# Softmax over the dilated groups on compact columns, with only the shares spread over the channels

## What is computed

```python
o = jnp.stack(outs, axis=2)
alpha = jax.nn.softmax(jnp.stack(lses, axis=2), axis=2)
o = (o * alpha[..., None].astype(o.dtype)).reshape(B, S, DIL_WIDTH)
return o * jax.nn.silu(g)
```

```python
w = jnp.exp(-DECAY_SCALE * jax.nn.sigmoid((w0 + jnp.tanh(wd) @ w_up).astype(f32)))
a = jax.nn.sigmoid((a0 + ad @ a_up).astype(f32))
kk = kk / jnp.maximum(jnp.linalg.norm(kk, axis=-1, keepdims=True), 1e-12)
k = k * (1.0 + (a - 1.0) * per_head(k_a))
```

## Time and profile before

| | |
|---|---|
| median of 3 runs | 2264.72 us (2263.03 to 2273.73) |
| the profiled execution | 2263.61 us, its span 2261.8 us |
| mean granted TensorE clock | 0.958 |
| PE busy | 2076.3 us (92%) |
| DVE busy | 956.5 us (42%) |
| ACT busy | 440.8 us (19%) |
| POOL busy | 239.7 us (11%) |

### The profile page before, as it was taken

The page is one execution under the profiler, slowest core; times in us unless marked ns, Lnnn a source line. Parts: engine busy times, 40 slices in busy tenths (PEclk is TensorE's granted clock), DMA queues, the critical chain, the costliest instruction groups (busy, mean ns, idle before and its releaser), DMA issues. The chain is left out here.

```text
span 2261.8 us, 31372 instructions
## 1 busy us (share of the span) xinstructions
PE 2076.3 (92%) x12841; PEld 1026.2 (45%) x12841; DVE 956.5 (42%) x1773; ACT 440.8 (19%) x877; POOL 239.7 (11%) x193
## 2 busy tenths in 40 slices
PE   7989898999998998999899997989799799999998
PEld 3553345643463343564444543536444444444443
DVE  1049668551116778853333561493321511111112
ACT  1011342121002144121312342401111100000000
POOL 0030410000011140000004540500000000000000
PEclk9999999999999999999899998998899899999999
DMA  4125110111214401112102101121146399999997
GB/s 163 70 110 204 47 40 25 50 66 65 88 50 169 175 10 40 36 38 86 58 19 75 57 19 55 49 84 40 38 149 262 138 401 420 420 420 421 420 420 316
DMA packets 63177, 328.93 MB, mean 145 GB/s; under 512 B 7248, under 2 KB 9808, under 8 KB 34640
## 3 DMA queue, kind: packets, MB, share of 16 engines
q1 hardware_dynamic: 63056, 327.22, 37.5%
HBM read 320.11 MB, written 6.29 MB: 144 GB/s over the span
## 5 line engine op out<-in xcount | busy, mean ns | idle before, releaser
L434 PE MATMUL ps<-store,side_ring 128*128 128x512 f32 x824 | 407.7, 624 | 14.9 <-DMA side_ring<-in_w_rwkv 6.5
L434 PEld LDWEIGHTS ps<-store,side_ring 128*128 128x128 f32 x824 | 146.0, 194 | 188.7 <-issue 168.8
L2596 PE MATMUL ps<-expert_ring,xe 128*64 128x512 f32 x1024 | 223.3, 593 | 3.7 <-DMA expert_ring<-in_w_expert 1.9
L347 PE MATMUL ps<-store,side_ring 128*128 128x512 f32 x384 | 168.3, 601 | 1.9 <-DVE store L313 1.9
L2596 PEld LDWEIGHTS ps<-expert_ring,xe 128*64 128x64 f32 x1024 | 72.9, 137 | 150.6 <-issue 148.6
L434 PE MATMUL ps<-store 128*128 128x512 f32 x256 | 119.1, 622 | 12.3 <-DMA store<-in_w_merge 10.4
L347 PEld LDWEIGHTS ps<-store,side_ring 128*128 128x128 f32 x384 | 74.1, 193 | 95.0 <-issue 92.5
L2624 PE MATMUL ps<-expert_ring,store 128*64 128x512 f32 x512 | 113.0, 600 | 1.4 <-DVE store L2681 1.4
L1664 PE MATMUL ps<-store,raw 128*128 128x512 f32 x256 | 110.7, 593 | 1.9 <-DVE store L313 1.9
L2653 ACT ACTIVATE store<-ps 128x1024 f32<-128x1024 f32 x16 | 16.4, 1025 | 418.0 <-PE ps L2596 418.0
L2668 DVE SCALAR_TENSOR_TENSOR x<-ps,mod,x 128x512 f32<-128x512 f32 x64 | 48.1, 751 | 109.0 <-PE ps L2573 104.6
(11 more groups left out here) (430 smaller groups left out, 3047.4 us busy)
## 6 DMA issues: line engine op xcount, KB each, us to landing
expert_ring<-in_w_expert SPq DMA_DIRECT2D x192, 1024.0 KB, 16.8
mixed<-in_w_ada SPq DMA_DIRECT2D x24, 1024.0 KB, 4.9
side_ring<-in_w_attn SPq DMA_DIRECT2D x32, 512.0 KB, 3.8
side_ring<-in_w_rwkv SPq DMA_DIRECT2D x20, 512.0 KB, 4.4
raw<-in_ple_gate SPq DMA_DIRECT2D x16, 512.0 KB, 4.9
store<-in_w_merge SPq DMA_DIRECT2D x16, 512.0 KB, 3.9
side_ring<-in_w_conv SPq DMA_DIRECT2D x12, 512.0 KB, 3.5
gates_before<-gated SPq DMA_DIRECT2D x16, 256.0 KB, 2.0
```

What stands on the lines that cost most here:

```text
L347: last = nc.tensor.matmul(ps[:, u, :], ring[:, u, k, :], src[:, k, :], start=(k == 0), stop=(k == kt - 1))
L434: ins = self.nc.tensor.matmul(self.ps[:, self.banks[j % banks], :], self.ring[:, j % self.slots, k, :], self.src[:, k, :], start=(k == 0), ...
L2596: last = nc.tensor.matmul(ps[w, 2 * ep + half, :], xe[:, ep, k, :], ring[:, unit % SLOTS, k2, S * half:S * half + S], start=(k == 0), stop ...
```

## The change

The softmax is done on the compact columns, and only its result is spread.

- `lse` of groups 1 and 2 is copied into `later` (four residues by two groups by two heads, 16 columns). A matrix `mover` of 515 columns has ones where column 3 + 4i meets partition i. A window of it 128 columns wide, at 128 t + 3 - r, moves the values of residue r to the partitions of the tokens of tile t. Sixteen products of 128x128 by 128x4, accumulated over the residues, bring `later` into token order (`moved`, 16 columns of PSUM bank 3). GpSimd, idle here before, writes `mover`.
- TensorE does these products behind the raise products, and waits for all six sigmoids, for `mover` and for `lse` first; bank 3 is one of the banks that the sigmoids read. The norm products, which also go to bank 3, wait for the three centred groups.
- Maximum, differences, exponential, sum and reciprocal work on 8 or 24 columns. One product over 24 columns gives the shares. The six diagonals are made of the shares, and the six spreads stand on TensorE behind the spreads of the norms. The copy of the first group to SBUF is gone.
- The gate is multiplied into the attention output before the spread arrives, then the spread shares are multiplied from PSUM: six wide products instead of nine.
- ScalarE's exponential of the shares stands ahead of those of the decays.

The table memory `M.tables` holds `mover` and the compact columns in place of the wide shares.

```diff
@@ -1187,11 +1187,15 @@
     r, k, v = z[:, R_R:R_R + 3, :], z[:, R_K:R_K + 3, :], z[:, R_V:R_V + 3, :]
     keep, lse, stay = sbt("keep", [P, RP]), sbt("lse", [P, 24]), sbt("stay", [P, RP])
     logw, cum, rate, tmp, grow = (sbt(x, [P, RP, S]) for x in ("logw", "cum", "rate", "tmp", "grow"))
-    diag, first, top = room[:, 0:6, :], room[:, 6, :], room[:, 7, :]
-    share, total = M.tables[:, 0:3, :], M.tables[:, 3, :]
+    diag = room[:, 0:6, :]
+    mover, share = M.tables[:, 0:2, :].rearrange("p u n -> p (u n)")[:, 0:S + 3], M.tables[:, 2, 0:24]
+    top, total = M.tables[:, 2, 24:32], M.tables[:, 2, 32:40]
+    later = M.tables[:, 2, 40:56]
+    per_group = lambda ap: ap.rearrange("p (g c) -> p g c", g=3)
+    moved = ps[:, 3, 0:16].rearrange("p (t g j) -> p g t j", t=4, g=2)
...
@@ -1212,15 +1216,16 @@
                     pe.wait_ge(s["sig_done"], i - 3)
                 nc.tensor.matmul(ps[:, 3 + i % 4, :], up[w, j * P:(j + 1) * P], z[w, R_WA, :], start=True,
                                  stop=True).then_inc(s["raised"], 1)
+            pe.wait_ge(s["sig_done"], 2 * RP)
+            pe.wait_ge(s["mover_ready"], 1)
+            pe.wait_ge(s["lse_ready"], 1)
+            for t in range(4):
+                for r in range(4):
+                    last = nc.tensor.matmul(ps[:, 3, 4 * t:4 * t + 4], mover[:, P * t + 3 - r:P * t + 3 - r + P], later[:, 4 * r:4 * r + 4],
+                                            start=(r == 0), stop=(r == 3))
+            last.then_inc(s["moved"], 1)
             gates.multiply(pe, KT)
-            for g in range(3):
-                for j in range(2):
-                    pe.wait_ge(s["diag_ready"], 2 * g + j + 1)
-                    row = ps[HD * j:HD * j + HD, g, :]
-                    out = row.rearrange("p (t i) -> p t i", t=4) if g == 0 else row.rearrange("p (i r) -> p r i", r=4)
-                    nc.tensor.matmul(out, M.c("ones")[:, 0:HD], diag[:, 2 * g + j, :].rearrange("p (t i) -> p t i", t=4),
-                                     start=True, stop=True).then_inc(s["group_spread"], 1)
-            pe.wait_ge(s["sig_done"], 2 * RP)
+            pe.wait_ge(s["centred"], 3)
             for j in range(RP):
                 pe.wait_ge(s["squares"], j + 1)
                 nc.tensor.matmul(ps[32 * j:32 * j + 32, 3, :], M.c("head_rows"), tmp[:, j, :], start=True,
@@ -1231,6 +1236,11 @@
                 w = slice(32 * j, 32 * j + 32)
                 nc.tensor.matmul(ps[:, kk_bank[j], :], M.c("head_spread")[w, :], norms[w, :], start=True,
                                  stop=True, tile_position=(32 * j, 0)).then_inc(s["kk_spread"], 1)
+            for g in range(3):
+                for j in range(2):
+                    pe.wait_ge(s["diag_ready"], 2 * g + j + 1)
+                    nc.tensor.matmul(ps[HD * j:HD * j + HD, g, :], M.c("ones")[:, 0:HD], diag[:, 2 * g + j, :],
+                                     start=True, stop=True).then_inc(s["group_spread"], 1)
             gates.multiply(pe, gates.products)
             pe.wait_ge(s["combined"], 3)
             pe.wait_ge(s["gate_raw"], RP)
@@ -1254,21 +1264,25 @@
                 nc.scalar.activation(tmp[:, j, :], at[:, j, :], ACT.Square).then_inc(s["squares"], 1)
             act.wait_ge(s["stay_ready"], 1)
             gates.take(act, 1)
-            act.wait_ge(s["group_spread"], 6)
-            nc.scalar.activation(first, ps[:, 0, :], ACT.Copy).then_inc(s["first_ready"], 1)
             act.wait_ge(s["normed"], RP)
             nc.scalar.activation(norms, ps[0:32 * RP, 3, :], ACT.Sqrt).then_inc(s["root"], 1)
+            act.wait_ge(s["centred"], 3)
+            nc.scalar.activation(share, share, ACT.Exp).then_inc(s["share_exp"], 1)
             act.wait_ge(s["log_ready"], 1)
             nc.scalar.activation(tmp[:, :, :], cum[:, :, :], ACT.Exp, scale=-DECAY_SCALE).then_inc(s["exps"], 1)
             nc.scalar.activation(grow[:, :, :], cum[:, :, :], ACT.Exp, scale=DECAY_SCALE).then_inc(s["exps"], 1)
-            act.wait_ge(s["centred"], 3)
-            nc.scalar.activation(share, share, ACT.Exp).then_inc(s["share_exp"], 1)
             nc.scalar.activation(logw[:, :, :], logw[:, :, :], ACT.Exp, scale=-DECAY_SCALE).then_inc(s["exps"], 1)
             gates.take(act, RP)
             for j in range(RP):
                 act.wait_ge(s["gate_raw"], j + 1)
                 nc.scalar.activation(z[:, R_G + j, :], raw[:, R_G + j, 1:S + 1], ACT.Identity,
                                      scale=stay[:, j:j + 1]).then_inc(s["gate_kept"], 1)
+
+        @block.gpsimd
+        def _(pool):
+            nc.gpsimd.memset(mover, 0.0).then_inc(s["mover_clear"], 1)
+            pool.wait_ge(s["mover_clear"], 1)
+            nc.gpsimd.tensor_copy(mover[:, 3:3 + S].rearrange("p (i r) -> p i r", r=4)[:, :, 0], M.c("ident")).then_inc(s["mover_ready"], 1)
 
         @block.vector
         def _(dve):
@@ -1280,44 +1294,47 @@
                 V.tensor_scalar(at[:, j, :], k[:, j, :], col("k_k", j), None, ALU.mult).then_inc(s["kk_made"], 1)
             dve.wait_ge(s["logs"], 1)
             own.step(V.tensor_tensor(lse[:, :], lse[:, :], maxima, ALU.add))
-            for g in range(3):
-                for j in range(2):
-                    c = lse[:, 8 * g + j:8 * g + j + 7:2].unsqueeze(2).broadcast_to([P, 4, P])
-                    V.tensor_tensor(diag[:, 2 * g + j, :].rearrange("p (t i) -> p t i", t=4),
-                                    M.c("ident").unsqueeze(1).broadcast_to([P, 4, P]), c, ALU.mult).then_inc(s["diag_ready"], 1)
+            V.tensor_copy(later.rearrange("p (r g j) -> p g r j", r=4, g=2),
+                          lse[:, 8:24].rearrange("p (g r j) -> p g r j", g=2, r=4)).then_inc(s["lse_ready"], 1)
             dve.wait_ge(s["sig_done"], 2 * RP)
             for j in range(RP):
                 V.tensor_scalar(bt[:, j, :], rate[:, j, :], col("k_a", j), keep[:, j:j + 1], ALU.mult,
                                 ALU.add).then_inc(s["scale_ready"], 1)
+            by_tile = lambda ap: ap.rearrange("p (t j) -> p t j", t=4)
+            sources = (by_tile(lse[:, 0:8]), moved[:, 0], moved[:, 1])
+            dve.wait_ge(s["moved"], 1)
+            own.step(V.tensor_tensor(by_tile(top), sources[0], sources[1], ALU.max))
+            own.step(V.tensor_tensor(by_tile(top), by_tile(top), sources[2], ALU.max))
+            for g in range(3):
+                V.tensor_tensor(by_tile(share[:, 8 * g:8 * g + 8]), sources[g], by_tile(top), ALU.subtract).then_inc(s["centred"], 1)
             for j in range(RP):
                 own.mark(V.tensor_tensor_scan(cum[:, j, :], M.c("chunk_carry"), logw[:, j, :], 0.0, ALU.mult, ALU.add))
             own.settle()
             V.tensor_tensor(logw[:, :, :], cum[:, :, :], logw[:, :, :], ALU.subtract).then_inc(s["log_ready"], 1)
             dve.wait_ge(s["scale_ready"], RP)
             own.mark(V.tensor_tensor(k, k, bt[:, :, :], ALU.mult))
-            dve.wait_ge(s["first_ready"], 1)
-            own.step(V.tensor_tensor(top, first, ps[:, 1, :], ALU.max))
-            own.step(V.tensor_tensor(top, top, ps[:, 2, :], ALU.max))
-            for g in range(3):
-                V.tensor_tensor(share[:, g, :], ps[:, g, :], top, ALU.subtract).then_inc(s["centred"], 1)
             dve.wait_ge(s["root"], 1)
             own.step(V.tensor_scalar(norms, norms, 1e-12, None, ALU.max))
             V.reciprocal(norms, norms).then_inc(s["inv_norm"], 1)
             dve.wait_ge(s["share_exp"], 1)
-            own.step(V.tensor_tensor(total, share[:, 0, :], share[:, 1, :], ALU.add))
-            own.step(V.tensor_tensor(total, total, share[:, 2, :], ALU.add))
+            own.step(V.tensor_tensor(total, share[:, 0:8], share[:, 8:16], ALU.add))
+            own.step(V.tensor_tensor(total, total, share[:, 16:24], ALU.add))
             own.step(V.reciprocal(total, total))
+            own.step(V.tensor_tensor(per_group(share), per_group(share), total.unsqueeze(1).broadcast_to([P, 3, 8]), ALU.mult))
+            for g in range(3):
+                for j in range(2):
+                    c = share[:, 8 * g + j:8 * g + j + 7:2].unsqueeze(2).broadcast_to([P, 4, P])
+                    V.tensor_tensor(diag[:, 2 * g + j, :].rearrange("p (t i) -> p t i", t=4),
+                                    M.c("ident").unsqueeze(1).broadcast_to([P, 4, P]), c, ALU.mult).then_inc(s["diag_ready"], 1)
             for j in range(RP):
                 dve.wait_ge(s["kk_spread"], j + 1)
                 V.tensor_tensor(at[:, j, :], at[:, j, :], ps[:, kk_bank[j], :], ALU.mult).then_inc(s["kk_ready"], 1)
             for g in range(3):
-                own.mark(V.tensor_tensor(share[:, g, :], share[:, g, :], total, ALU.mult))
+                own.mark(V.tensor_tensor(od[:, g, :], od[:, g, :], dg[:, g, :], ALU.mult))
             own.settle()
             for g in range(3):
-                own.mark(V.tensor_tensor(share[:, g, :], share[:, g, :], od[:, g, :], ALU.mult))
-            own.settle()
-            for g in range(3):
```

(9 more changed lines are left out.)

## The result

The changed kernel takes 2273.82 us (median of 7 runs, 2269.13 to 2275.23); the kernel before, beside it on the same chip, 2264.94 us (7 runs, 2262.11 to 2273.73). The ratio is 1.0028, 95% interval 1.0016 to 1.0040. The median lies above the range of the forecast. The profiled execution took 2274.9 us.

The account below looks back on a forecast made before the run. In the changed phase VectorE was taken as nearly full, TensorE close behind. The terms gave -1.8 and -2.9 us by layer, -4.7 together: 2263.61 to 2258.9, and 1.1 for the median made 2260.0, range 2255.5 to 2270.

Parts of the forecast that it names:

- The step that failed: Small TensorE products behind the last sigmoid: priced at 3.63 us from an earlier row of the same form.
- term two: Way from last sigmoid to the norms' reciprocal, with small products in front: +0.75 us first layer, -0.35 second.
- first rival: TensorE's clock falls at small products (+3.5 us) and gate projection behind (+2.4): 5.9 us a layer, slower; chance 0.22.
- Term one: VectorE from the norms' reciprocal to the last combined head: 12.71 us becomes 10.14, -2.57 us a layer.
- What must hide: GpSimd's preparation ready 2.1 us ahead of the last sigmoid; TensorE's later list ending 0.5 us before VectorE's last addition.
- Rival two: TensorE bounds the phase's end: later third gate projection, output products beginning at half clock (+2.4 us); 2262.6; chance 0.13.
- Rival four: Small products cheaper than the 3.63 us row, down to 1.0 us: 2254 to 2257; chance 0.06.
- Rival three: Phase shortens but later stages wait for their own transfers, worth 0 to -2 us: 2263.6; chance 0.09.

Follow-up runs that it names:

- e1: The changed kernel with the first gate projection put back ahead of the small products: 2271.48 us, ratio 1.0026 to the kernel before.
- e2: The changed kernel with small products in bank 0, right behind the raise products, without the wait for the sigmoids: 2267.92 us, ratio 1.0006 to the kernel before.
- e6: The changed kernel with each small product's moving operand repeated 32 times, 128 columns instead of 4: 2267.78 us, ratio 1.0002 to the kernel before.
- e8: The kernel before, with only a wait for all six sigmoids added ahead of the first gate projection: 2272.30 us, ratio 1.0025.
- e11: The changed kernel with small products in bank 0, no wait for the sigmoids, and 128 columns wide: 2260.47 us, ratio 0.9978 to the kernel before.
- e9: The kernel before with 128 semaphore increments added to TensorE's list in the first phase: 2281.50 us, ratio 1.0070.
- e10: The changed kernel with small products behind the norms, 128 columns wide, plus 128 semaphore increments in the first phase: 2269.70 us, ratio 1.0015 to the kernel before.
- e5: The kernel before, unchanged, run again for a second profile: 2269.13 us, ratio 1.0009.
- e3: The changed kernel with the sixteen small products done twice: 2289.77 us, ratio 1.0098 to the kernel before.

## Why the prediction was wrong

**The step that failed** is "I take 3.63 because the shape is the same, at full clock", with the gate projection at 7.07 behind it. The shape was the same, the place was not. The earlier trace rows stood behind dense passes, and e1 shows that there 3.63 is right (and that the price then comes behind it, 8.83 for 7.13); behind 1.19 us of idle the group took 6.10 and the projection 9.74, so 2.47 + 2.67 = 5.1 us were missing from term two, in both layers. That is the first rival, whose price (3.5 + 2.4 = 5.9) was close; it was given 0.22. (The 2.4 rests on a misreading: 6.7 us was the length of the stretch asked for in the earlier trace rows, while the ten output products took 7.33 in the earlier trace rows against 4.45 at full clock, so 2.9. The projection lost 2.67.) Its condition, "1 us of idle and 3.5 us of passes that stream 4 columns", was on paper; e2, e6, e8 and e11 show that the narrow passes are the cause, with 3.3 us of the loss, and that the idle only adds to them. The argument against the rival, a clock of 1.00 while L2069 ran, came from one execution, and nothing dense follows that row (two passes, then 5.75 us of idle), so it could not show the price behind it. What in the wider passes keeps the clock up, the columns read or those written, was not separated. The rule of the Trainium skill, "TensorE: Matmul & The Clock Gate", Part 1, that the default state is throttled and activity releases it, spoke for that rival. The trace agrees as far as the clock fell to 0.50 from 327.60 and came back during dense passes; but the prediction took the gap for the danger, and without the gap the clock fell too (e2: 0.71 from 326.50, 0.50 from 328.00).

The other steps:
- **Term one, -2.57 us a layer**: right, and a little low. From reciprocal to last combined head 9.85 us instead of 12.71: -2.86.
- **Term two**, +0.75 and -0.35 us, was +5.80 and +4.69. Without the clock it was right: 22.2 - 5.1 = 17.1 us, the forecast's 17.15.
- **What must hide**: GpSimd was ready 4.7 us ahead of the last sigmoid (forecast 2.1). VectorE's wait ahead of the root is 4.66 us, well above the 2.5 forecast at most, because the root came late: without the 2.67 of the slow projection it is 2.0.
- **Rival two** is out. The output products begin at full clock, 10 passes in 4.53, behind 0.73 us of idle (forecast 0.8); after the reciprocal VectorE doesn't wait.
- **Rival four** is out: no run had the group below 3.63.
- **Rival three** was right in kind. It said that later stages could take back what the phases gain, by 0 to 2 us, for loads asked for behind a barrier. The rest grew by 5.5 us; e9 and e10 show one such place, 1.6 us of it. Its mechanism, packets of instruction code on the load, wasn't foreseen.

The first rival's own number was 2270.7 with both layers hit. The phases grew by 2.94 + 1.31 = 4.25 us and the wait for `in_w_z` by 1.60, together 5.9, which on 2263.61 gives 2269.5; the profiled execution took 2274.9. **What stays open** is the other 5.4 us of that one: 1.6 lie ahead of and between the two phases, the others in the rest beside the wait. Part of it is scatter: medians of one kernel differ by 3.7 us (e5), and the ratio, 1.0028, makes 6.3 us of the medians' 8.9. Part comes from the rest of the program: it was 1342.9 to 1343.2 us in the two executions of the kernel before, 1347.8 to 1350.0 in the seven experiments that carry the change's instructions once, but 1349.90 in e8 too, which has no such instruction and no long wait for `in_w_z`. The stretch from 1357 to 1450 ran at a lower clock in e3, e8, e9 and e10 (0.83 to 0.87, against 0.91 in the kernel before). e3 and e10, with 256 instructions more and phases of 63 and 49 us, have the same rest to 0.1 us (1354.95, 1354.90), so the length of the changed phases is not what lengthens it; why it grows was not tried. That the wait for `in_w_z` follows the count of instructions is shown (0.45, 2.32; 2.19, 0.62), and so is the packet beside the load; that this packet and nothing else delays it is argued.

## What to carry to other kernels

Before a run of tiny products is put on TensorE, price what comes behind it too: 32 passes of 4 columns, busy without a gap by the profile, cost their weight loads and then 1.6 to 2.6 us in the dense group that follows. Where the weight load sets the pace anyway, widen the moving operand until it fills that time (4 to 128 columns cost 0.1 to 0.2 us here), and put the run behind dense work and behind what the critical chain waits for. A duration from a row holds with its neighbours: read what stood ahead of the row, what came behind it, and at which clock it ran. When a product is moved on one engine, look again at the order of the queue that waits for it: in e1 the other engine's own order took the gain away.

## What the runs showed of the hardware

- A pass with its own load of 128 columns starts every 0.11 us at 2.4 GHz and some 0.2 us at 1.2 GHz (32 in 3.63; 64 in 13.81), with 4 columns moved as with 128 (3.84).
- TensorE's busy share says nothing of the clock: 100% by weight loads in the stretch from 327.60, granted clock 0.50.
- 32 such passes with 4 columns, without any idle ahead, saw the granted clock fall from 1.00 to 0.50 before they ended (e2); with 128 columns they took 3.84 us and the group behind them kept full pace (e11).
- 1.19 us of idle left a full clock full (7.13 behind it); 0.78 us of idle at a low clock made the projection 9.20 us instead of 7.82 (e8).
- 128 increments of a semaphore on TensorE ended the first phase 8.3 us later, 0.065 us for each. That is a lower bound of what one takes: the phase lasted 12.4 us without them, and some may have run beside its wait for the constants.
- 128 TensorE instructions more, in the first phase (e9) or in the changed ones, moved a wait near 1540 us from 0.45 to 2.0 to 2.4 us, and 128 more on top of the change's moved it back to 0.6 (e10).
